# Sixteen more tokens of an expert layer through gathered rows, with the v products turned so that tokens are the moving operand

## What is computed

```python
def rms_norm(x, gain):
    xf = x.astype(jnp.float32)
    y = xf * lax.rsqrt(jnp.mean(xf * xf, axis=-1, keepdims=True) + EPS)
    return (y * gain.astype(jnp.float32)).astype(x.dtype)
...
def peer_ffn(h, w_query, sub_keys, expert_u, expert_v):
    """PEER product-key expert retrieval. h (T, D) -> (T, D)."""
    T, D = h.shape
    qry = (h @ w_query).reshape(T, P_HEADS, 2, P_HALF)
    scores = jnp.einsum("thcd,hcnd->thcn", qry, sub_keys).astype(jnp.float32)
    s_top, i_top = lax.top_k(scores, P_TOPK)
    cand_s = (s_top[:, :, 0, :, None] + s_top[:, :, 1, None, :]).reshape(T, P_HEADS, P_TOPK * P_TOPK)
    cand_i = (i_top[:, :, 0, :, None] * N_KEYS + i_top[:, :, 1, None, :]).reshape(T, P_HEADS, P_TOPK * P_TOPK)
    best_s, best_pos = lax.top_k(cand_s, P_TOPK)
    expert_idx = jnp.take_along_axis(cand_i, best_pos, axis=-1)
    gates = jax.nn.softmax(best_s, axis=-1).astype(h.dtype)
...
        act = jax.nn.gelu(jnp.einsum("td,thkd->thk", hb, expert_u[eb]), approximate=False)
        return jnp.einsum("thk,thkd->td", act * gb, expert_v[eb])
...
        h = rms_norm(x, g_pre_ffn[l]) * (1.0 + scale2) + shift2
        y = peer_ffn(h.reshape(B * S, D), w_query[l], sub_keys[l], expert_u[l], expert_v[l]).reshape(B, S, D)
        x = x + gate2 * rms_norm(y, g_post_ffn[l])
```

## Time and profile before

| what | us |
|---|---|
| median of 3 runs (1991.05 to 1993.48) | 1992.89 |
| span of the profiled execution | 1990.5 |
| up to the first dense u matmul | 822.9 |
| u steps 0 to 59, with routing (822.9 to 1082.1) | 259.2 |
| u steps 60 to 107, with one-hot work (1082.1 to 1367.9) | 285.8 |
| u steps 108 to 127 (1367.9 to 1460.3) | 92.3 |
| v steps (1460.3 to 1984.5) | 524.2 |
| from the last v matmul to the end | 6.0 |

### The profile page before, as it was taken

How to read it: one execution, slowest core, us unless ns; L and a number is a source line. 1 busy time by engine, 2 the same in 40 slices (tenths; PEclk the granted TensorE clock), 3 DMA queues, 4 the chain that set the end, 5 groups by cost and what they waited for, 6 DMA issues and landing times.

```text
span 1990.5 us, 27945 instructions
## 1 busy us (share of the span) xinstructions
PE 1935.9 (97%) x10357; PEld 1710.3 (86%) x10357; DVE 1497.9 (75%) x2735; ACT 723.5 (36%) x1331; POOL 420.1 (21%) x231
## 2 busy tenths in 40 slices
PE   7999999999999999999999999999999999999998
PEld 4789777889877988999999999999988888888887
DVE  4776645364576537788889999996688898889986
ACT  4110233010351343343443444444444444444443
POOL 0333211444102023001111511111221222222210
PEclk9999999999999999999999999999999999999999
DMA  7235311353112432257668688888999999999993
GB/s 276 86 115 195 121 56 40 130 200 117 63 43 85 149 106 85 95 171 273 226 217 276 221 319 303 300 304 299 397 387 401 401 400 401 399 401 395 402 378 131
DMA packets 212644, 465.94 MB, mean 234 GB/s; under 512 B 15625, under 2 KB 157121, under 8 KB 193345
## 3 DMA queue, kind: packets, MB, share of 16 engines
q1 hardware_dynamic: 193408, 330.43, 47.7%
q0 software_dynamic: 18432, 134.23, 17.1%
q10 hardware_dynamic: 704, 0.04, 0.0%
HBM read 410.12 MB, written 54.53 MB: 233 GB/s over the span
## 4 chain that ended last, share of the span: by engine, by line
PE 43%; DMA 9%; DVE 4%; ACT 1%; issue 1%; SPq 1%; DVEq 0%; POOLq 0%; POOL 0%; ACTq 0%
PE xin_ps_u L2148 22%; PE xin_out L2192 16%; DMA experts_hot<-act_scratch 6%; PE xin_out L2170 4%; DMA con_raw<-in_expert_u 2%; DMA con_raw<-in_expert_v 1%; DVE over_v_vlo L2453 1%; DVE in_ulo L2304 1%; DVE experts_acc L1960 1%; SPq L2120 1%; DVE experts_rows L1941 1%; DVE xin_wt L2450 0%; ACT in_uhi L2221 0%; DVE xin_wlo L2455 0%; ACT L2263 0%
## 5 line engine op out<-in xcount | busy, mean ns | idle before, releaser
L1934 POOL DMA_INDIRECT experts_rows<-in_expert_rows,experts_idx x128 | 204.7, 1599 | 915.7 <-DVE experts_acc L1960 779.3
L2148 PE MATMUL xin_ps_u<-con_h_hi,in_uhi 128*128 128x384 f32 x1024 | 349.0, 341 | 11.3 <-DVE in_ulo L2304 9.1
L2148 PE MATMUL xin_ps_u<-con_h_hi,in_ulo 128*128 128x384 f32 x1024 | 343.3, 335 | 0.0
L2148 PE MATMUL xin_ps_u<-con_h_lo,in_uhi 128*128 128x384 f32 x1024 | 343.2, 335 | 0.0
L2192 PE MATMUL xin_out<-over_v_vhi,xin_whi 128*128 128x512 f32 x768 | 238.7, 389 | 2.3 <-DVE xin_wlo L2455 2.2
L2192 PE MATMUL xin_out<-over_v_vhi,xin_wlo 128*128 128x512 f32 x768 | 238.5, 389 | 0.0
L2192 PE MATMUL xin_out<-over_v_vlo,xin_whi 128*128 128x512 f32 x768 | 238.4, 389 | 0.0
L2304 DVE TENSOR_TENSOR in_ulo<-con_raw,in_uhi 128x1024 fp32r<-128x1024 f32 x127 | 155.2, 1222 | 81.2 <-ACT in_uhi L2221 78.7
L2148 PEld LDWEIGHTS xin_ps_u<-con_h_hi,in_uhi 128*128 128x128 f32 x1024 | 193.2, 189 | 15.6 <-DVE in_ulo L2304 13.0
L2148 PEld LDWEIGHTS xin_ps_u<-con_h_lo,in_uhi 128*128 128x128 f32 x1024 | 193.3, 189 | 0.0
L2148 PEld LDWEIGHTS xin_ps_u<-con_h_hi,in_ulo 128*128 128x128 f32 x1024 | 192.9, 188 | 0.0
(11 more groups left out here) (445 smaller groups left out, 3738.5 us busy)
## 6 DMA issues: line engine op xcount, KB each, us to landing
con_raw<-in_expert_u SPq DMA_DIRECT2D x128, 512.0 KB, 4.7
con_raw<-in_expert_v SPq DMA_DIRECT2D x128, 512.0 KB, 11.9
con_raw<-in_w_in SPq DMA_DIRECT2D x36, 1024.0 KB, 6.2
act_scratch<-in_act SPq DMA_DIRECT2D x128, 192.0 KB, 2.2
experts_hot<-act_scratch SPq DMA_DIRECT2D x128, 192.0 KB, 12.1
gate_scratch<-in_stage SPq DMA_DIRECT2D x12, 1024.0 KB, 7.2
gate_scratch<-over_s_stage SPq DMA_DIRECT2D x12, 1024.0 KB, 8.0
experts_hot<-gate_scratch SPq DMA_DIRECT2D x16, 768.0 KB, 14.0
```

The source lines that it names most:

```text
L1934: pool.indirect_dma_start(out=self.rows[:, r % ROWS, :], out_offset=None, in_=table, in_offset=at).then_inc(self.row_in[r % ROWS], 16)
L2148: mm = pe.matmul(ps_u[s % 2][:, 0:TD], a[s % 2][:, k, :], m[:, k, P:T], start=(i == 0), stop=(i == 3 * KD - 1))
```

## The change

Sixteen tokens of the second tile (`XT`) leave the dense passes and go by gathered rows. The 128 slots of each of these tokens are laid in eight groups of sixteen slots on eight groups of sixteen partitions, so that sixteen more gathers of 128 rows (`XSLOTS`) serve them all: 144 slots in place of 128. For that

- h of these tokens is turned by 16 matmuls after u step 1 (`turn_extra`), kept by ScalarE and copied by seven DMAs to the other groups of partitions at SP's step 8; their indices and gates are moved by 16 small DMAs at SP's step 34 (`X_MOVE`), behind a wait for the routing of the second tile;
- the partial sums of the eight groups are brought together by seven DMAs and seven adds at v steps 120 and 121, and normed and added to x on steps 122 to 125;
- the dense passes work on 368 columns (`TN`) in place of 384, the one-hot steps are 46 (steps 58 to 103) in place of 48, the steps in between 2 in place of 4, the tail 24 in place of 20;
- the slots stand at other places: 10 on u steps 24 to 57, 23 on the one-hot steps, 24 on the tail (every step), 87 on v steps 0 to 113.

The v products are turned: v is stationary, eight blocks of 128 of the width, and the weighted product of 368 tokens is the moving operand, so a v step is 24 matmuls of 368 columns into eight banks in place of 18 of 512 into six. The result stands transposed. At the end each bank is scaled by gain (VectorE) and squared (ScalarE), the squares are added on VectorE and summed over partitions by three matmuls with ones, the banks are turned back by 24 transposes (`turn_chunk`), and after one power for all tokens (POOL) six operations add the result to x.

```diff
@@ -1978,19 +1996,20 @@
     inside = [[] for n in range(NEXP)]
     r = 0
     for n in range(N_SEARCH + R_STEPS + 4, NEXP):
-        if (n < N_ROUTE and n % 4 == 0) or N_ROUTE <= n < N_HOT0 or (N_HOT0 <= n < N_HOT0 + N_HOT and n % 2 == 0) or (n >= N_HOT0 + N_HOT and n % 4 != 3):
+        if (n < N_ROUTE and n % 4 == 0) or N_ROUTE <= n < N_HOT0 or (N_HOT0 <= n < N_HOT0 + N_HOT and n % 2 == 0) or n >= N_HOT0 + N_HOT:
             inside[n].append(r)
             r += 1
     outside = [[] for n in range(NEXP)]
-    left, over = SLOTS - r, NEXP - 8
+    left, over = ALL_SLOTS - r, END - 2
     for n in range(over):
         if (n + 1) * left // over > n * left // over:
             outside[n].append(r)
             r += 1
...
+END = NEXP - 12
 IN_AT, OUT_AT = slots_of_steps()
...
                 every(n)
+                if n == 8:
+                    sp.wait_ge(hx_kept, 2)
+                    for q in range(1, XQ):
+                        sp.dma_start(hx[q * XT:(q + 1) * XT], hx[0:XT]).then_inc(hx_spread, 16)
+                if n == X_MOVE:
+                    sp.wait_ge(x_idx, 1)
+                    sp.wait_ge(chosen, 2 * STAGES)
+                    for q in range(XQ):
+                        rows, some = slice(q * XT, (q + 1) * XT), slice(q * XSLOTS, (q + 1) * XSLOTS)
+                        sp.dma_start(got.idx[rows, SLOTS:ALL_SLOTS], flat(idx_x)[0:XT, some]).then_inc(got.extra_in, 16)
+                        sp.dma_start(got.gate[rows, SLOTS:ALL_SLOTS], flat(gate[1])[0:XT, some]).then_inc(got.extra_in, 16)
...
+            def turn_extra():
+
+                for half in range(2):
+                    for j in range(4):
+                        k = 4 * half + j
+                        for i in range(2):
+                            mm = pe.matmul(ps_h[half][:, j * P:(j + 1) * P], as_f32(hT[i][:, k, P:2 * P]), con.ident[:],
+                                           start=(i == 0), stop=(i == 1))
+                    mm.then_inc(hx_turned, 1)
+
             for n in range(N_HOT0):
                 every(n, n)
+                if n == 1:
+                    turn_extra()
...
-            kinds = ((whi, vhi), (whi, vlo), (wlo, vhi))
-            product = lambda s, t, h, w, m, **flags: pe.matmul(
-                out[t][h][:], w[s][:, t * P:(t + 1) * P], m[s][:, h * 512:(h + 1) * 512], **flags)
+            kinds = ((vhi, whi), (vhi, wlo), (vlo, whi))
+            product = lambda s, k, v, w, **flags: pe.matmul(
+                bank[k][:, 0:TN], v[s][:, k * P:(k + 1) * P], w[s][:], **flags)
             for it in pairs(pe, NEXP // RING - 1, True):
                 for s in range(RING):
                     n = RING * it + s
                     first = isinstance(n, int) and n == 0
                     prepared(n)
-                    for t in range(ND):
-                        for i, (w, m) in enumerate(kinds):
-                            for h in range(2):
-                                mm = product(s, t, h, w, m, start=(first and i == 0), stop=False)
+                    for k in range(KD):
...
+                        for i, (v, w) in enumerate(kinds):
+                            mm = product(s, k, v, w, start=(first and i == 0), stop=False)
                     mm.then_inc(used, 1)
...
+            def turn_chunk(k):
+
+                pe.wait_ge(kept_t, max(k, 3 * (k // 4) + 2) + 1)
+                pe.wait_ge(sq_done, 3 * (k // 4) + 3)
+                for t, (c0, c1) in enumerate(PIECE):
+                    mm = pe.transpose(turned_out[t][k // 4][0:c1 - c0, k % 4 * P:(k % 4 + 1) * P], y_t[k][:, c0:c1],
+                                      con.ident[:])
+                mm.then_inc(turned, 1)
+
+            for k in range(KD):
+                for s in range(RING):
+                    if k == 0:
+                        prepared(NEXP - RING + s)
+                    for i, (v, w) in enumerate(kinds):
+                        mm = product(s, k, v, w, start=False, stop=(s == RING - 1 and i == 2))
+                mm.then_inc(closed, 1)
+                for j in {4: (0, 1, 2), 5: (3,), 7: (4, 5, 6)}.get(k, ()):
+                    turn_chunk(j)
+            turn_chunk(KD - 1)
+            pe.wait_ge(added, KD - 1)
+            for t, (c0, c1) in enumerate(PIECE):
+                mm = pe.matmul(ps_ss[:, t:t + 1], ssq[:, c0:c0 + P], con.ones[:, 0:1], start=True, stop=True)
+            mm.then_inc(ss_done, 1)
```

The last part of VectorE's program, in the new order:

```diff
+            def add_square(k):
+
+                dve.wait_ge(sq_done, k + 1)
+                wait(dve, added, k - 1)
+                dve.tensor_tensor(ssq[:], ssq[:], sq[k % 2][:], ALU.add).then_inc(added, 1)
+
+            for k in range(KD):
+                dve.wait_ge(closed, k + 1)
+                dve.tensor_scalar(y_t[k], bank[k][:, 0:TN], con.gate_b[:, k:k + 1], None, ALU.mult).then_inc(kept_t, 1)
+                if k > 1:
+                    add_square(k - 1)
+            add_square(KD - 1)
+            dve.wait_ge(ss_done, 1)
+            dve.tensor_scalar(ms[:], ps_ss[:, 0:ND], 1.0 / D, EPS, ALU.mult, ALU.add).then_inc(ms_done, 1)
+            dve.wait_ge(pow_done, 1)
+            dve.wait_ge(turned, KD)
+            for m in range(2 * ND):
+                t, (c0, c1), half = m // 2, PIECE[m // 2], slice(m % 2 * 512, (m % 2 + 1) * 512)
+                dve.scalar_tensor_tensor(out=x[0:c1 - c0, t + 1, half], in0=turned_out[t][m % 2][0:c1 - c0, :],
+                                         scalar=rstd[0:c1 - c0, t:t + 1], in1=x[0:c1 - c0, t + 1, half],
+                                         op0=ALU.mult, op1=ALU.add).then_inc(dve_sum, 1)
+
```

More of the change, by code:

```diff
@@ L1729 @@
 U_RING, R_STEPS, G_STEPS, G_TOK = 4, 12, 16, 8
+XT = 16
 TD = T - P
 ND = TD // P
+DENSE = slice(XT, TD)
+TN = TD - XT
 SLOTS = PH * TOPK
+XQ = P // XT
+XSLOTS = SLOTS // XQ
+ALL_SLOTS = SLOTS + XSLOTS
 ROWS = 4
@@ L1944, in weigh @@
     def weigh(self, act, r):
+        if r == SLOTS:
+            act.wait_ge(self.extra_in, 32 * XQ)
         act.wait_ge(self.dot_done, r + 1)
@@ L1998, with experts_block @@
 G_RUN = 4 * 8 * G_TOK
-def experts_block(nc, con, ring, hot, hot_all, stage, early, got, rt, A, hT, acts, gmat, x1, dst, vhi, vlo, cut_hi, cut_lo):
+def experts_block(nc, con, ring, hot, hot_all, stage, early, got, rt, A, hT, acts, gmat, x1, dst, vhi, vlo, cut_hi, cut_lo, vacant):
     u = A["expert_u"]
@@ L2263, in _ @@
                     act.activation(ge, eg, ACT.Exp).then_inc(exp_done, 1)
+                if n == 2:
+                    for half in range(2):
+                        act.wait_ge(hx_turned, half + 1)
+                        act.activation(hx[0:XT, 4 * half:4 * half + 4, :], ps_h[half][0:XT, :].rearrange("p (k n) -> p k n", n=P),
+                                       ACT.Copy).then_inc(hx_kept, 1)
+                if n == N_HOT0:
+                    act.wait_ge(chosen, STAGES * NT)
+                    act.activation(stage[0][:, :, 0:XT], con.iota[:].unsqueeze(2).to_broadcast([P, NK, XT]),
+                                   ACT.Copy).then_inc(blank, 1)
                 if N_HOT0 <= n < N_HOT0 + N_HOT:
-                    gates((n - N_HOT0) // G_STEPS, (n - N_HOT0) % G_STEPS)
+                    gates((n - N_HOT0 + HOT_SKIP) // G_STEPS, (n - N_HOT0 + HOT_SKIP) % G_STEPS)
             for n in range(NEXP):
@@ L2522, in experts @@
-def experts(nc, con, slots, ring, A, hT, x1, acts, gmat, out, begun):
+                if n == END + 5:
+                    dve.wait_ge(moved_in, 16 * (XQ - 1))
+                    for q in range(1, XQ):
+                        wait(dve, moved_sum, q - 1)
+                        dve.tensor_tensor(acc_x[0:XT], acc_x[0:XT], moved[q - 1], ALU.add).then_inc(moved_sum, 1)
+                if n == END + 7:
+                    dve.wait_ge(ss0_done, 2)
+                    dve.tensor_scalar(ms0[0:XT, 1:2], ss0[0:XT, 1:2], 1.0 / D, EPS, ALU.mult, ALU.add).then_inc(ms0_done, 1)
@@ new lines, in _, with experts @@
+            for m in range(2 * ND):
+                t, (c0, c1), half = m // 2, PIECE[m // 2], slice(m % 2 * 512, (m % 2 + 1) * 512)
+                dve.scalar_tensor_tensor(out=x[0:c1 - c0, t + 1, half], in0=turned_out[t][m % 2][0:c1 - c0, :],
+                                         scalar=rstd[0:c1 - c0, t:t + 1], in1=x[0:c1 - c0, t + 1, half],
+                                         op0=ALU.mult, op1=ALU.add).then_inc(dve_sum, 1)
+def experts(nc, con, slots, ring, A, hT, x1, acts, gmat, out, begun, vacant):
@@ L2558, in build_program @@
         con = Consts(al)
+        with Alloc(nc, "over_h") as ah:
+            vacant = [ah.sb(f"vacant{i}", [P, KD, T]) for i in range(2)]
         hT = al.sb("h_hi", [P, KD, T], F32R), al.sb("h_lo", [P, KD, T], F32R)
```

245 lines of the change are left out of this document (136 added, 109 removed).

## The result

The changed kernel takes 2046.0 us (median of four runs, 2044.8 to 2047.1), the kernel before 1992.3: a ratio of 1.026, 95% interval 1.025 to 1.028. It is slower by 53.7 us; the forecast was 2032 us, 39.1 us over the 1992.9 known then, with 2004 to 2052 as the range. The profiled execution of after has a span of 2045.2 us, 0.8 us under the median.

A forecast was written before the change was run, and what follows sets the result against it. TensorE bounds most of the kernel, VectorE nearly as full in one-hot steps, DMA neck and neck in v steps. Stages 250 + 267.3 + 123.5 + 555.6 + 10 = 1206.4 us against 1167.6, +38.8: 2032 us, range 2004 to 2052.

The forecast's parts named there:

- What decides C and D: Last u steps and v steps: DMA is full there and sets the time, not TensorE; chance 0.80.
- C: Last u steps, now 24 instead of 20: 123.5 us against 92.3, from 48.2 MB at 391 GB/s.
- D: The 128 v steps: 555.6 us against 524.2, with 114 steps at 4.35 us and 14 at 4.00.
- The first rival: Last u steps and v steps: DMA has room, v steps take 4.00 us; 1985 us, faster by 0.4%; chance 0.08.
- A: Dense u steps beside routing, before the one-hot work, now 58 instead of 60: 250 us against 259.2.
- The sixteen small DMAs: Dense u steps: issues of about 0.33 us each on SP's queue delay a u load; 3 us, ends 0 and 8.
- The turning of h: Dense u steps: sixteen matmuls for the extra tokens, priced like the one-hot ones at 1.78 us.
- the other waits: Dense u steps: waits where routing on VectorE is longer than a step, put at 13 us.
- B: U steps with one-hot work, now 46 instead of 48: 267.3 us against 285.8, VectorE the bound at 5.81 us a step.
- E: The end, behind the last v matmul: 10 us against 6.0, with 2.4 us from the last operation to the span's end.
- The bunched waits: V steps: waits gather and leave TensorE at 1.2 GHz, costing up to 27 us; 2059 us; chance 0.05.

The follow-up runs named there:

- the spread kernel: The changed kernel with its sixteen small DMAs issued two behind each u load of steps 37 to 44, not all behind step 34's load: 2036.0 us, ratio 1.021.
- the kernel with short operations: The changed kernel with dot and add of the sixteen extra slots on 8 of 1024 columns, gathers moving as many bytes: 2043.4 us, ratio 1.025.

## Why the prediction was right, point by point

The time lies in the range, 14 us over the forecast. The stages below make 14.9 us, the span up to the first u step, where nothing was changed, 1.0; and the median lies 0.8 us over the profiled span, not 2.4.

**What decides C and D** was right: removing the gathers (41.5 us back), adding them to before (D +37), changing TensorE's work (none in the first 114 v steps) and VectorE's (none there), taking other bytes out (44.5 us back), and taking twelve gathers out of C (C 14.1 us shorter) all fall as the sum of bytes says. The first rival needed a mean of 438 GB/s; no run here goes over 400 in those 400 us. The page "DMA: Bandwidth & Descriptors" of the Trainium skill gives 358 GB/s of HBM to a core in its Specifications, as half of a stack's 716; the kernels of this study whose 400 us are shown above ran on one core at 394 to 400, so the measurement decides.

**A, 250 forecast, 258.3 measured.** Two terms of its sum were too small. The sixteen small DMAs: I took 3 us, with 8 as the end. The load left at 971.5 and not 964.8 us, since the issues took 10.3 us and not 5.3 and began at 961.2 and not 959.5; it landed after 6.9 us and not 4.7. TensorE stopped for 8.8 us and then ran 6.8 us at 1.2 GHz (granted 0.5). In the spread kernel A is 10.4 us shorter. The turning of h: I priced its sixteen calls at the 1.78 us of the one-hot row, but such a call leaves two records in the trace, and the x16 of that row counts records: a one-hot step has eight calls, not sixteen. Step 1 took 7.49 us where its neighbours take 4.08 and 4.09, so 3.4 us. The two overruns are 10.4 - 3 = 7.4 us, by the A of the spread kernel, and 1.6, and the other waits came to 0.7 less than the 13 I had put: together 8.3.

**B, 267.3 against 266.8.** The time was right, the bound is in doubt. VectorE was to be it and is 99% busy, but the chain of after goes through TensorE's matmuls without a gap, 5.79 us a step, and TensorE waited for VectorE for 0.3 us in the whole stage:

```profile
1098.63 1.78 PE xin_bank L2225 x16
1100.41 4.00 PE xin_bank L2203 x24
```

The forecast had the two 0.02 us a step apart (5.79 and 5.81), so the time cannot tell which it is; that it came out is no sign for VectorE.

**C, 123.5 against 116.7.** Right in its cause, too long by 6.8: 46.3 MB went through the stretch at 397 GB/s, not 48.2 at 391. Of its 24 gathers 22 were issued within it, 2.1 MB less.

**D, 555.6 against 568.5.** The bytes were right, the rate and the end were not. 504.15 us x 392 GB/s are 197.6 MB, 1.733 MB a step (forecast 1.751); at 400 that is 4.33 us, at 392 it is the 4.42 measured. So 8.2 of the 12.9 us are in the first 114 steps, and the term that was too small is the rate. I had read 400 off the middle 400 us and taken it for all; over its first 120 v steps the kernel before ran at 394 itself (398 and 392 in the earlier trace rows), at a share of 1.03. At 394 the bytes of after take 501.5 us, an estimate from these numbers, so some 3 us are a rate lower than that of before. The 4.42 is a mean, too: 13 of the 114 steps took 5.1 to 7.6 us, and 58 less than 4.2. The other 4.6 us are in the last 14 steps, 64.3 us against 59.7: TensorE was idle for 3.5 us there (2.5 forecast) and its clock fell to half for 6.8 us behind two waits of 2.2 and 1.3 us, 3.4 us lost that no term had; the twelve transposes there took 1.6 us for 1.2. These waits have no fixed price: with the same program in them, the last 14 steps took 59.8 us in the kernel with short operations and 60.8 in the one with the spread moves. Steps 114 to 123 ran at 4.02 us, as forecast.

**E, 10 against 11.0.** Right but for the last store. The operations ahead of it in after:

```profile
2037.98 4.04 DVE L2637 SCALAR_TENSOR_TENSOR xin_x<-xin_bank,xin_rstd,xin_x 112x512 f32<-112x512 f32 x6 [0.99 <-POOL xin_rstd L2393]
```

The six operations end at 2042.02, the span at 2045.20: 3.2 us behind them, not 2.4.

**The bunched waits** (third rival) came in part: TensorE's clock fell to half three times in the first 114 v steps, for 3.4 us each. For the most part DMA went on meanwhile, as the prediction had it: its share is 1.02 in the mean. Not wholly: in the slices from 1760 and 1870 us, right behind waits of 3.5 and 2.7 us with such a spell, the share is 0.95 and 0.99 and the rate 348 and 358 GB/s. By these slices that is some 2 us of bytes, an estimate. The waits mattered more in A and in the last 14 steps, where DMA is not the bound.

## What to carry to other kernels

Price an edit in each stage by the resource that is full there: here the same gather cost 2.2 to 2.8 us in the v steps, where DMA is full, and 1.4 us among the routing steps, where it is not, and matmuls saved in a stage that DMA sets are not collected at all. Here bytes that were added to one queue slowed the other where the sum of the queues' shares was 1.03, so add up MB per step against the rate of the same stretch before moving work from an engine to DMA. And count every small DMA on a queue that also carries loads: sixteen in a row stopped TensorE for 8.8 us, two per step, begun a little later, did not.
